# SSM stage of a hybrid decoder step: the token transposes of x split over the second z projection, the B by C products moved inside the third

## The reference, cut to what matters

```python
def step(S, inp):                     # one block of 128 tokens of one group
    xc, dtc, Bc, Cc = inp
    cum = jnp.cumsum(dtc * a_coef, axis=1)
    decay = jnp.exp(jnp.where(tri, cum[:, :, None] - cum[:, None, :], -jnp.inf))
    cb = jnp.einsum('bign,bjgn->bijg', Cc, Bc)
    y = jnp.einsum('bijgh,bjghp->bighp', cb[..., None] * decay * dtc[:, None], xc)
    y = y + jnp.einsum('bign,bghpn->bighp', Cc, S) * jnp.exp(cum)[..., None]
    wb = dtc * jnp.exp(cum[:, -1][:, None] - cum)
    S = S * jnp.exp(cum[:, -1])[..., None, None] + jnp.einsum('bjgh,bjgn,bjghp->bghpn', wb, Bc, xc)
    return S, y
# after it: y += d_skip * x, y *= silu(z), y is divided by the root mean square over each group's 512 channels
```

## Time and profile before

| | before |
|---|---|
| median of three executions | 1745.52 us (1744.14 to 1749.04) |
| the profiled execution | 1744.65 us, its span 1743.0 us |
| busy, share of the span | PE 96%, its weight loads 81%, DVE 44%, ACT 23%, POOL 23% |
| mean granted TensorE clock | 0.987 |
| the SSM stage, four groups | about 60 to 476 us of the span |
| TensorE busy in it, 60 to 510 us | 432.99 of 450 us, DVE 287.08 |

### The profile page before, as it was taken

The page is one execution under the profiler, slowest core; times in us unless marked ns, Lnnn a source line. Parts: engine busy times, 40 slices in busy tenths (PEclk is TensorE's granted clock), DMA queues, the critical chain, the costliest instruction groups (busy, mean ns, idle before and its releaser), DMA issues.

```text
span 1743.0 us, 25870 instructions
## 1 busy us (share of the span) xinstructions
PE 1674.6 (96%) x10438; PEld 1413.3 (81%) x10438; DVE 761.0 (44%) x1312; ACT 407.9 (23%) x800; POOL 405.7 (23%) x344
## 2 busy tenths in 40 slices
PE   8999999999999999999899999999996999999995
PEld 6777677777877777787677777779995999999995
DVE  5657677675341212111212212244477871067334
ACT  2252432524212121121011111133224111111122
POOL 0041131402220000000233211003444334433432
PEclk9999999999999999999999999999998999999998
DMA  5324224252362222221778765333231222223221
GB/s 187 137 90 146 89 79 154 79 178 83 105 204 78 61 72 63 72 65 37 232 238 253 243 236 209 138 141 110 85 97 37 96 87 85 85 88 95 85 61 52
DMA packets 70410, 206.24 MB, mean 118 GB/s; under 512 B 10161, under 2 KB 26802, under 8 KB 65682
## 3 DMA queue, kind: packets, MB, share of 16 engines
q1 hardware_dynamic: 50384, 151.67, 26.8%
q10 hardware_dynamic: 13762, 31.93, 5.2%
q0 software_dynamic: 6144, 20.98, 3.9%
HBM read 189.68 MB, written 14.86 MB: 117 GB/s over the span
## 4 chain that ended last, share of the span: by engine, by line
PE 88%; DVE 6%; DMA 2%; ACT 2%; issue 1%; SPq 1%; POOLq 0%; POOL 0%; ACTq 0%; DVEq 0%
PE acc L1711 31%; PE acc L1751 29%; PE acc L2044 6%; PE acc L2010 3%; PE acc L1992 2%; PE acc L2147 1%; PE bank L2059 1%; DVE work L1212 1%; PE bank L2078 1%; PE bank L2060 1%; PE bank L2161 1%; PE bank L2029 1%; PE bank L2035 1%; PE bank L2232 1%; PE bank L1913 1%
## 5 line engine op out<-in xcount | busy, mean ns | idle before, releaser
L1711 PE MATMUL acc<-xt,ring 128*128 128x272 f32 x2272 | 545.8, 398 | 2.7 <-DMA ring<-in_stream 2.7
L1711 PEld LDWEIGHTS acc<-xt,ring 128*128 128x128 f32 x2272 | 429.9, 191 | 103.7 <-issue 17.7
L1751 PE MATMUL acc<-x_parts,f_parts 128*128 128x272 f32 x1408 | 219.6, 291 | 13.3 <-DVE x_parts L1141 11.4
L522 POOL TENSOR_TENSOR f_parts<-ring,f_parts 128x1024 fp32r<-128x1024 f32 x65 | 157.6, 2424 | 247.9 <-ACT f_parts L701 247.7
L1751 PEld LDWEIGHTS acc<-x_parts,f_parts 128*128 128x128 f32 x1408 | 196.1, 191 | 15.8 <-issue 8.0
L500 POOL DMA_DIRECT2D work<-in_page_cols x128 | 68.8, 538 | 476.1 <-PE bank L2099 367.0
L1751 PE MATMUL acc<-f_parts 128*128 128x272 f32 x1344 | 172.3, 289 | 0.0
L1751 PEld LDWEIGHTS acc<-f_parts 128*128 128x128 f32 x1344 | 170.4, 188 | 0.1
L701 ACT ACTIVATE f_parts<-ring 128x1024 fp32r<-128x1024 f32 x65 | 69.0, 1061 | 238.4 <-PE acc L1751 204.2
L2044 PE MATMUL acc<-branch,ring 128*128 128x272 f32 x512 | 120.0, 392 | 0.0
L2044 PEld LDWEIGHTS acc<-branch,ring 128*128 128x128 f32 x512 | 96.0, 190 | 18.8
(11 more groups left out here) (351 smaller groups left out, 2051.1 us busy)
## 6 DMA issues: line engine op xcount, KB each, us to landing
ring<-in_stream SPq DMA_DIRECT2D x216, 512.0 KB, 3.6
work<-in_page_cols POOLq DMA_DIRECT2D x128, 160.0 KB, 3.3
attended<-in_ssm_state ACTq DMA_DIRECT2D x8, 1024.0 KB, 6.3
work<-cum_rows SPq DMA_DIRECT2D x32, 256.0 KB, 4.6
out_ssm_s<-attended ACTq DMA_DIRECT2D x8, 1024.0 KB, 5.7
work<-in_ckv_rows ACTq DMA_DIRECT2D x64, 128.0 KB, 3.4
work<-in_ckv_rows SPq DMA_DIRECT2D x64, 128.0 KB, 2.9
work<-in_memk_cols SPq DMA_DIRECT2D x8, 1024.0 KB, 6.7
```

The source lines that it names most:

```text
L522: pool.tensor_tensor(lo, ring[:, s * BLOCK:(s + 1) * BLOCK], hi.bitcast(F), SUB).then_inc(sem["split_ready"], 1)
L1711: m = pe.matmul(acc[p][:, half, 0:width], w[:, k * P:(k + 1) * P], x(kk)[:, half * width:(half + 1) * width], start=kk == 0, stop=kk == n_ ...
L1751: m = pe.matmul(acc_half, w[:, k * P:(k + 1) * P], x[:, kk, of], start=kk == 0 and n == 0, stop=kk == last and n == 2)
```

## The change

TensorE turns x in three parts: blocks 0 and 1 where all were turned before, blocks 2 and 3 between the halves of z block 1, the samples behind z block 1. The products of B and C move from the place ahead of z block 2 to between its halves. VectorE reads blocks 0 and 1, gates z block 0, reads blocks 2 and 3, takes the reciprocal of the previous group's root (split off `group_norm` as `group_reciprocal`), reads the samples, and goes on as before. No arithmetic is added or left out.

```diff
@@ -1264,10 +1264,12 @@
                             4 * RMS_EPS, MUL, ADD)
                 m.then_inc(sem["g_var_ready"], 1)
 
-            def group_norm(g):
+            def group_reciprocal():
                 dve.wait_ge(sem["g_std_ready"], t.next("g_std_ready"))
                 dve.reciprocal(rstd, rstd).then_inc(sem["dve_step"], 1)
                 dve.wait_ge(sem["dve_step"], t.next("dve_step"))
+
+            def group_norm(g):
                 for hp in range(GC):
                     dve.scalar_tensor_tensor(out=BR[:, g * GC + hp, :], in0=BR[:, g * GC + hp, :],
                             scalar=V("ssmg", g * GC + hp), in1=rstd, op0=MUL, op1=MUL)
@@ -1276,23 +1278,29 @@
                 finish(g, QC - 1)
                 if g:
                     group_var()
-                for c in range(NB + 1):
-                    n = rows_of(c)
-                    dve.wait_ge(sem["x_turned"], t.next("x_turned"))
-                    ps = by_head(bank[c % 2][0:n, :])
-                    dve.tensor_tensor(by_head(xdt[0:n, c, :]), ps, heads(dt_tm, c, g, n), MUL)
-                    if c < NB:
-                        dve.tensor_tensor(by_head(xw[:, c, :]), ps, heads(wb_tm, c, g, n),
-                                MUL).then_inc(sem["turned_read"], 1)
-                ps, wb_s = by_head(bank[NB % 2][0:NS3, :]), heads(wb_tm, NB, g, NS3)
-                if g:
-                    dve.wait_ge(sem["adds_ready"], t.value("adds_ready"))
-                dve.tensor_tensor(by_head(xw_full), ps[NS:2 * NS], wb_s[NS:2 * NS], MUL)
-                dve.tensor_tensor(by_head(xw_s), ps, wb_s, MUL).then_inc(sem["turned_read"], 1)
-                t.skip("turned_read", NB)
-                dve.wait_ge(sem["turned_read"], t.next("turned_read"))
-                dve.tensor_tensor(xw_s[NS:2 * NS, :], xw_full, xw_s[NS:2 * NS, :].bitcast(F),
-                        SUB).then_inc(sem["xw_s_ready"], 1)
+                def turned(*cs):
+                    for c in cs:
+                        n = rows_of(c)
+                        dve.wait_ge(sem["x_turned"], t.next("x_turned"))
+                        ps = by_head(bank[c % 2][0:n, :])
+                        dve.tensor_tensor(by_head(xdt[0:n, c, :]), ps, heads(dt_tm, c, g, n), MUL)
+                        if c < NB:
+                            dve.tensor_tensor(by_head(xw[:, c, :]), ps, heads(wb_tm, c, g, n),
+                                    MUL).then_inc(sem["turned_read"], 1)
+
+                def turned_samples():
+                    turned(NB)
+                    ps, wb_s = by_head(bank[NB % 2][0:NS3, :]), heads(wb_tm, NB, g, NS3)
+                    if g:
+                        dve.wait_ge(sem["adds_ready"], t.value("adds_ready"))
+                    dve.tensor_tensor(by_head(xw_full), ps[NS:2 * NS], wb_s[NS:2 * NS], MUL)
+                    dve.tensor_tensor(by_head(xw_s), ps, wb_s, MUL).then_inc(sem["turned_read"], 1)
+                    t.skip("turned_read", NB)
+                    dve.wait_ge(sem["turned_read"], t.next("turned_read"))
+                    dve.tensor_tensor(xw_s[NS:2 * NS, :], xw_full, xw_s[NS:2 * NS, :].bitcast(F),
+                            SUB).then_inc(sem["xw_s_ready"], 1)
+
+                turned(0, 1)
 
                 def z_gate(hp):
                     a = (hp + 1) % 2
@@ -1306,6 +1314,10 @@
                     dve.tensor_tensor(d, d, cb_p.rearrange("p c n -> p (c n)"), MUL).then_inc(sem["decay_ready"], 1)
 
                 z_gate(0)
+                turned(2, 3)
+                if g:
+                    group_reciprocal()
+                turned_samples()
                 if g:
                     group_norm(g - 1)
                 dve.wait_ge(sem["b_tm_read"], t.next("b_tm_read"))
@@ -1866,17 +1879,20 @@
                 pe.wait_ge(sem["conv_ready"], t.next("conv_ready", QC))
                 if g:
                     pe.wait_ge(sem["pair_read"], t.next("pair_read", 2))
-                for c in range(NB + 1):
-                    if c >= 2:
-                        pe.wait_ge(sem["turned_read"], t.next("turned_read"))
-                    for f in range(GC):
-                        x = toks(BR[:, g * GC + f, :], c)
-                        if c < NB:
-                            m = pe.transpose(bank[c % 2][:, f * P:(f + 1) * P], x, C("ident"))
-                        else:
-                            for third in thirds:
-                                m = pe.matmul(bank[c % 2][third, f * P:(f + 1) * P], x, C("ident"), start=True, stop=True)
-                    m.then_inc(sem["x_turned"], 1)
+                def turn(*cs):
+                    for c in cs:
+                        if c >= 2:
+                            pe.wait_ge(sem["turned_read"], t.next("turned_read"))
+                        for f in range(GC):
+                            x = toks(BR[:, g * GC + f, :], c)
+                            if c < NB:
+                                m = pe.transpose(bank[c % 2][:, f * P:(f + 1) * P], x, C("ident"))
+                            else:
+                                for third in thirds:
+                                    m = pe.matmul(bank[c % 2][third, f * P:(f + 1) * P], x, C("ident"), start=True, stop=True)
+                        m.then_inc(sem["x_turned"], 1)
+
+                turn(0, 1)
                 if g:
                     pe.wait_ge(sem["g_var_ready"], t.next("g_var_ready"))
                 for c in range(NB):
@@ -1884,13 +1900,17 @@
                 for third in thirds:
                     m = pe.matmul(bank[3][third, 0:P], toks(B, NB), C("ident"), start=True, stop=True)
                 m.then_inc(sem["b_turned"], 1)
-                project(0, of_x)
-                pe.wait_ge(sem["turned_read"], t.next("turned_read", 2))
-                for c in range(NB):
-                    pe.matmul(bank[0][:, c * P:(c + 1) * P], toks(B, c), toks(C_, c), start=True, stop=True)
-                m = pe.matmul(bank[1][0:NS, 0:NS], toks(B, NB), toks(C_, NB), start=True, stop=True)
-                m.then_inc(sem["cb_ready"], 1)
-                project(1, of_x)
+                project(0, of_x, between=lambda: turn(2, 3))
+                turn(4)
+
+                def b_by_c():
+                    pe.wait_ge(sem["turned_read"], t.next("turned_read", 2))
+                    for c in range(NB):
+                        pe.matmul(bank[0][:, c * P:(c + 1) * P], toks(B, c), toks(C_, c), start=True, stop=True)
+                    m = pe.matmul(bank[1][0:NS, 0:NS], toks(B, NB), toks(C_, NB), start=True, stop=True)
+                    m.then_inc(sem["cb_ready"], 1)
+
+                project(1, of_x, between=b_by_c)
                 pe.wait_ge(sem["b_tm_read"], t.next("b_tm_read"))
                 for c in range(NB):
                     if c >= 2:
```

## The result

The changed kernel takes 1732.72 us (median of four executions, 1731.09 to 1734.73) against 1744.83 us: a ratio of 0.9931, with a 95% interval of 0.9911 to 0.995. In eight further executions the ratio was 0.9943 (0.9925 to 0.9962), or 10.0 us. The profiled execution went from 1744.65 to 1732.98 us, its span from 1743.0 to 1731.3.

A forecast was written before the change was run, and what follows sets the result against it. TensorE, busy for 96% of the span, was taken as the bound, with VectorE deciding groups 1 to 3; gains of 2.30 + 2.36 + 1.36 + 1.36 = 7.4 us gave 1738.1 us, range 1733.6 to 1743.3.

The forecast's parts named there:

- The wait that was removed: Turn of x: TensorE waits for VectorE's reads of the same two banks; 2.90 us of stall in group 2.
- The price of a half: Each half of split z blocks 1 and 2 on TensorE: taken as 3.80 us, with 3.67 and 3.86 for the range.
- The new wait at the turn of B: Groups 1 to 3: TensorE waits for VectorE's group_var read of the banks; 0.2 us, between nothing and 0.3.
- the sum: Adding the new order's pieces per group, then the four groups' gains: 2.30 + 2.36 + 1.36 + 1.36 = 7.4 us.
- VectorE as the next bound: State additions, groups 1 to 3: VectorE free at 303.13, 0.92 us late for its copy; gain 1.36 us in group 2.
- The checks on the way: Samples read from their bank 0.7 us before TensorE wants it; products ready near 297.5, VectorE comes near 299.3.
- What lies outside the stretch: Other queues (DMA loads, GpSimd, ScalarE) and the stage's end: all put at nothing.
- h: Time of one half of a split projection on TensorE: 3.80 us, range 3.67 to 3.86; four in each group's stretch.
- Falls at the state additions: Rival: clock falls behind TensorE's longer wait there, 1.70 us in each of three groups; 1743.2 us, chance 0.12.
- given back at the sample additions: Rival: the chain ahead of them does not move with TensorE; groups 0 to 2 lose 6.0 us; 1744.1, chance 0.10.
- The new stops: Rival: eight more cuts in TensorE's projections each lose the clock once, 13.6 us against 7.4; 1751.7 us, chance 0.04.
- VectorE in time at the state additions: Rival: VectorE is not late, groups 1 to 3 gain more, 10.3 us in sum; 1735.2 us, chance 0.13.

The follow-up runs named there:

- both moves: Changed kernel with group_norm's scalings later in the group and VectorE's reads of the sample outputs ahead of finish(0): 1726.62 us, 0.9893 of the kernel before.
- both moves with filling: Changed kernel with scalings later, sample outputs read earlier, and 9 extra transposes in groups 0 to 2 ahead of the sample additions: 1724.91 us, ratio 0.989.

## Why the prediction was wrong, point by point

**The wait that was removed: right.** The turn of x held 2.9 us of stall in which two engines waited for each other in turn. The new places hide it whole, and no wait of L1889 for VectorE's reads is left. The price of a half was 3.77 us from start to start at all four places, against 3.80 taken from halves of 3.67 and 3.86. With 0.87 us instead of 0.90 for two blocks and 0.88 instead of 0.94 for B, the stretch came to 19.86 us instead of 20.12 in group 0.

**The new wait at the turn of B: right** in kind. The stretch is 0.30 us longer in groups 1 to 3 than in group 0, where the sum had 0.23, at the upper bound that it gave.

**VectorE as the next bound: right in mechanism, its size a little off.** It was to be free 22.40 us into the stretch; the copy began at 294.65 - 272.51 = 22.14. Four small steps of 0.05 to 0.07 us were each set too long: TensorE's way to block 2, the first read behind it (0.64 us after the transposes begin, not 0.71), a signal that cost nothing, and the copy, which begins 0.07 us before L1334 has ended. The new wait was 0.81 us against 0.92 of lateness. The gain was 1.68 us a group where 1.36 were forecast. Together, the order gave 7.6 us where the sum had 6.4 (7.4 less the 1.00 us of half clock). Taking the scalings out of VectorE's run removed the wait whole (0.82 us a group), which shows the cause.

**The checks on the way: right.** The samples are read 0.7 us before TensorE wants their bank, as in the sum (286.34 + 0.69 = 287.03 against 287.75). Putting the products back shows what that margin rests on: without the half of 3.77 us ahead of them TensorE waits for 3.04. Putting the reciprocal back shows the other side: ahead of the samples it fills a wait of VectorE, behind them it comes on top.

**What lies outside the stretch: the step that failed.** The sum put everything outside the four stretches at nothing, and took the falls of one profile as they stood. For the falls in the turn that was right on average by luck: 1.00 us in the sum, 0.95 in the mean over five profiles, but from 0 to 2.25 in single ones. For the rest it failed. In the first pair of profiles 3.0 of the 11.7 us lie outside the stretches: 1.9 behind z block 3's start, of which 1.7 is one slow half that the kernel before had in group 0 and the changed one had not, and 1.1 ahead of the stage. In the mean over five it is 1.3 us. Each execution draws its slow halves behind the wait of 2.1 us, 1.6 to 1.7 us apiece in one to three groups, and the part behind the stage ran from 1257.5 to 1261.6 us over the ten profiles. Single executions of one kernel therefore lie up to 12.7 us apart. The range had been built from the bounds of h and of VectorE's lateness alone, and this spread was in no term of it. By my estimate from these figures its low end, 1733.6, ought to have been some 2 us lower. The second part of the miss is the order, undersized by 1.2 us: 0.3 in group 0, from halves and small products that were each a little shorter, and 0.3 in each of the others, where VectorE was free earlier.

**The rivals.** Falls at the state additions did not come in the changed kernel: 0 in 15 stretches. They did come when the wait there was made 3.56 us. The gain was not given back at the sample additions: that wait is 2.1 us, before and after, so what starts it moved forward with TensorE. The new stops did not bring the clock down: none of 40 split projections in five profiles had a fall. The Trainium skill, "TensorE: Matmul & The Clock Gate", section on a second HAM failure mode, puts the oscillation down to brief idle times between groups of matmuls. That agrees with the waits of 2.1 us here, which a slow half followed in 17 of 30 cases; the new stops, which small matmuls fill without idle time, are not such a case. VectorE in time at the state additions, the rival on the fast side, was not the case either, until the scalings were moved; its 1735.2 us would have been nearer to the measured time than the forecast, for the wrong reason.

## What to carry to other kernels

When TensorE and VectorE take turns over two banks, put projections between the turns, and then follow VectorE's whole run of work to the next place where TensorE needs it: here the reciprocal and the products each had one right place, and either in its old one cost the entire gain. Look for falls of the clock behind every wait of TensorE, and take a difference between two kernels from stretches that repeat, from one start to the next, before trusting medians of a few executions. A wait that can't be removed may be cheaper if it is filled with matmuls whose result is thrown away: with both waits filled the kernel before took 1740.31 us against 1744.60.

## What the runs showed of the hardware

A fall costs up to 1.7 us when it meets a half of 16 matmuls (5.37 against 3.67), and 1.0 to 1.5 us in the turn of x (four cases). Behind the wait of 2.1 us in groups 0 to 2 it came in 17 of 30 cases over ten profiles of the two kernels. With the wait cut to about 1.3 us it came in none of 6 (sample outputs read earlier, both moves), and with it filled in none of 9 (the two kernels with this wait filled, both moves with filling). Up to 136 transposes whose results are thrown away made no kernel slower; the kernel before, with both waits filled, was faster for them by an interval that leaves out no difference, and for the changed one it can't be told. And the two engines' small instructions repeat so exactly, to 0.02 us over a stretch of 27 us, that a difference of a tenth can be read from a profile, while the time of the kernel hides one of several us.
